# The start of gate and up in a hybrid block: one wait and the order of two scaled rows

## The reference

```python
x = x + jnp.einsum('bse,ed->bsd', y, w_out[l])

h = rmsnorm(x, norm_ffn[l])
f = jax.nn.silu(jnp.einsum('bsd,df->bsf', h, w_gate[l])) * jnp.einsum('bsd,df->bsf', h, w_up[l])
x = x + jnp.einsum('bsf,fd->bsd', f, w_down[l])
return rmsnorm(x, norm_final)
```

## Time and profile before

| | us |
|---|---|
| median of 3 runs | 1904.69 |
| lowest and highest run | 1904.26, 1906.11 |
| span of the profiled execution, first to last instruction | 1902.7 |
| TensorE busy in it | 1875.1 |
| VectorE, ScalarE, GpSimd busy | 1106.6, 808.4, 1144.9 |

### The profile page before, as it was taken

The page is one execution under the profiler, slowest core; times in us unless marked ns, Lnnn a source line. Parts: engine busy times, 40 slices in busy tenths (PEclk is TensorE's granted clock), DMA queues, the critical chain, the costliest instruction groups (busy, mean ns, idle before and its releaser), DMA issues.

```text
span 1902.7 us, 22499 instructions
## 1 busy us (share of the span) xinstructions
PE 1875.1 (99%) x8374; PEld 1544.2 (81%) x8374; DVE 1106.6 (58%) x1269; ACT 808.4 (42%) x938; POOL 1144.9 (60%) x427
## 2 busy tenths in 40 slices
PE   9999999999999999999999999999999999999998
PEld 7888788877788788888888788888888888888886
DVE  6899988997645755455545854445443025433535
ACT  6466766585643533333333433333333222232235
POOL 3577477945734465666655755555555676676663
PEclk9999999999999999999999999999999999999999
DMA  6222132265777334533355433323333765655455
GB/s 196 78 79 88 45 100 78 75 224 172 247 240 231 117 125 127 153 119 127 112 153 176 151 105 114 106 88 105 115 105 127 288 225 190 210 189 211 166 198 221
DMA packets 240946, 284.20 MB, mean 149 GB/s; under 512 B 12095, under 2 KB 166207, under 8 KB 240364
## 3 DMA queue, kind: packets, MB, share of 16 engines
q1 hardware_dynamic: 240874, 283.25, 44.8%
q10 hardware_dynamic: 2, 0.00, 0.0%
HBM read 200.90 MB, written 82.31 MB: 149 GB/s over the span
## 4 chain that ended last, share of the span: by engine, by line
PE 82%; POOL 6%; DVE 5%; ACT 2%; issue 2%; DMA 2%; POOLq 0%; SPq 0%; DVEq 0%; ACTq 0%
PE ps L2133 19%; PE ps L2135 19%; PE ps L2134 19%; PE acc L2133 8%; PE acc L2135 8%; PE acc L2134 8%; DVE a_lo L1863 1%; POOL nsq L877 1%; PE ps L2161 1%; DVE t_sum L1887 1%; POOL nsq L879 1%; POOL w_lo L804 1%; POOL f_lo L1018 0%; DVE wo_lo L1707 0%; POOL glu L827 0%
## 5 line engine op out<-in xcount | busy, mean ns | idle before, releaser
L933 POOL TENSOR_TENSOR t_lo<-t_sum,t_hi 128x2048 fp32r<-128x2048 f32 x44 | 205.6, 4674 | 165.3 <-ACT t_hi L1366 165.2
L927 POOL TENSOR_TENSOR b_lo<-m_raw,b_hi 128x1536 fp32r<-128x1536 f32 x44 | 157.6, 3582 | 179.2 <-ACT b_hi L1361 121.9
L1018 POOL TENSOR_TENSOR f_lo<-f_raw,f_hi 128x2048 fp32r<-128x2048 f32 (+1 forms) x42 | 182.2, 4338 | 129.3 <-ACT f_hi L1518 124.8
L2133 PE MATMUL ps<-h_hi,w_hi 128*128 128x512 f32 x512 | 201.1, 393 | 0.8 <-POOL w_lo L804 0.8
L2135 PE MATMUL ps<-h_hi,w_lo 128*128 128x512 f32 x512 | 199.4, 389 | 0.0
L2134 PE MATMUL ps<-h_lo,w_hi 128*128 128x512 f32 x512 | 199.2, 389 | 0.0
L1887 DVE TENSOR_TENSOR t_sum<-m_raw 128x512 f32<-128x512 f32 x88 | 141.7, 1630 | 97.4 <-PE acc L2135 87.6
L1518 ACT CAST f_hi<-f_raw 128x2048 fp32r<-128x2048 f32 (+1 forms) x42 | 74.3, 1769 | 263.6 <-PE ps L2135 168.1
L2133 PE MATMUL ps<-wd_hi,f_hi 128*128 128x512 f32 x462 | 179.8, 389 | 0.8 <-POOL wd_lo L1025 0.8
L2134 PE MATMUL ps<-wd_lo,f_hi 128*128 128x512 f32 x462 | 179.7, 389 | 0.0
L2135 PE MATMUL ps<-wd_hi,f_lo 128*128 128x512 f32 x462 | 179.7, 389 | 0.0
(11 more groups left out here) (257 smaller groups left out, 4689.1 us busy)
## 6 DMA issues: line engine op xcount, KB each, us to landing
f_raw<-f_scr SPq DMA_DIRECT2D x35, 1024.0 KB, 4.9
wd_raw<-in_w_down SPq DMA_DIRECT2D x60, 512.0 KB, 6.6
f_scr<-fs SPq DMA_DIRECT2D x110, 256.0 KB, 2.1
m_raw<-in_w_gate SPq DMA_DIRECT2D x88, 256.0 KB, 3.9
m_raw<-in_w_up SPq DMA_DIRECT2D x88, 256.0 KB, 5.1
w_raw<-in_w_in SPq DMA_DIRECT2D x32, 512.0 KB, 5.3
f_scr<-gt SPq DMA_DIRECT2D x44, 256.0 KB, 2.0
xt<-in_x SPq DMA_DIRECT2D x16, 512.0 KB, 6.3
```

The costliest lines, as they stand in the source:

```text
L927: g.tensor_tensor(b_lo[b][:, :, :, :], m_raw[b][:, 0:3], f32(b_hi[b][:, :, :, :]), ALU.subtract).then_inc(s_mlo, 1)
L933: g.tensor_tensor(t_lo[b][:, :, :, :], t_sum[b][:, :, :, :], f32(t_hi[b][:, :, :, :]), ALU.subtract).then_inc(s_mlo, 1)
L1018: g.tensor_tensor(f_lo[j % 3][:, 0:n], f_raw[j % 2][:, 0:n], f32(f_hi[j % 3][:, 0:n]), ALU.subtract).then_inc(s_dlo, 1)
L2133: pe.matmul(bank, lhs[0](c), rhs[0](c), start=first, stop=False, skip_group_check=more)
```

## The change

Five edits in the lists above. GpSimd waits for VectorE's `a_low(4)` and `a_low(5)` before `b_lo` of matrix 1. VectorE scales row 14 before `sum11` (at the end of the loop over rows, behind `a_low(3)`), does `a_low(4)` and `a_low(5)` back to back, and scales row 15 behind them. ScalarE casts `a_high(6)` before it copies row 14 out. TensorE turns row 14 in the same place as before, but row 15 behind product 5 and not ahead of it. Nothing is added to or taken from the work itself.

```diff
--- before.py
+++ after.py
@@ -1032,6 +1032,7 @@
                     if h:
                         gate_block(first, FI, behind=A_LO_DVE[1, 4])
                     elif i == 0:
+                        pool.wait_ge(s_alo_dve, A_LO_DVE[0, 5])
                         raw_lo(1, 1)
                         pool.wait_ge(s_t, 8)
                         a_low(6)
@@ -1473,8 +1474,8 @@
                     raw_hi(m + 1, 1, i + 1)
                 copy_p5(m, i, 0, first)
                 if starts == 0:
+                    a_high(6)
                     h2_copy(NT - 2)
-                    a_high(6)
                 silu(i, 0, h)
                 copy_u2(m, i, 0, first)
                 if starts == 1:
@@ -1918,6 +1919,7 @@
                     add_row(w, first_weight_sums if w == NT - 1 else lambda: norm_between(w))
                 if w == NT - 1:
                     a_low(0, 3)
+                    row_scaled(NT - 2)
                 if w == 3:
                     row_scaled(2)
                 if w == 1 or 3 <= w < NT - 2:
@@ -1994,10 +1996,9 @@
 
                 if first and not b:
                     sum11(m, i, b, h, first)
-                    row_scaled(NT - 2)
-                    a_low(0, early[0])
+                    for n in early:
+                        a_low(0, n)
                     row_scaled(NT - 1)
-                    a_low(0, early[1])
                     dve.wait_ge(s_hn, NT)
                     for n in range(2):
                         dve.wait_ge(s_x2st[n], 16 * NT // 2)
@@ -2410,6 +2411,8 @@
                             between(n)
                         matrix_product(n, m + b, i, b, None if b else new_half, first)
                     if b == 0:
+                        if between:
+                            between(0)
                         matrix_product(0, m + 1, i, 1, None, first)
                     elif not last:
                         matrix_product(0, m + 2, i + 1, 0, next_half)
@@ -2417,8 +2420,10 @@
 
             def last_rows(n):
 
-                if n in (4, 5):
-                    turn_h2(NT - 6 + n)
+                if n == 4:
+                    turn_h2(NT - 2)
+                if n == 0:
+                    turn_h2(NT - 1)
                 if n == 2:
                     for e in range(2):
                         pe.wait_ge(s_outf[e], NT)
```

## The result

The changed kernel takes 1908.39 us (median of 21 runs, 1904.98 to 1912.31), the kernel before, run beside it, 1906.27 us (21 runs, 1903.57 to 1908.52). The ratio is 1.0013, interval 1.0007 to 1.0019. That is some 2 us slower (2.1 between the medians, 2.3 between the means), under 0.2%. The forecast was 1904.9, from 1902.7 to 1907.6, on the three runs then known.

What follows compares the result with a forecast made beforehand. TensorE, busy 1875.1 of 1902.7 us, bounds the kernel, with 4.94 us of holes here. The gain at product 4 is paid back at products 3, 5 and 6: +0.17 on 1904.69, forecast 1904.9, range 1902.7 to 1907.6.

Steps and rivals of the forecast that it cites:

- The turns and their sum: VectorE and GpSimd alternate under an exclusive lock; the reordered chain to a_lo6 makes product 6 0.17 us later.
- product 6: TensorE waits behind a_lo6 after product 0 of matrix 1: one hole of some 3.0 us, until 649.76.
- The hole before product 3: Product 3 of matrix 0 waits for sum11, now behind row 14: a new hole of 0.9 us.
- product 5: Product 5 of matrix 0 waits for ScalarE's copy of u2: 0.4 us of hole.
- row 15 held beside b_lo: Row 15's scaling waits its turn beside GpSimd's b_lo, over 3 us; rival, not held: 1903.7, chance 0.10.
- a_lo6 as the last link: a_lo6 on GpSimd, behind the weight sums, ends at 649.70 and releases product 6 0.06 us later.
- the covers of b_lo and of matrix 2: Slack before delays reach TensorE: 2.7 us for b_lo of matrix 1, 4.97 us for matrix 2.
- All later work moves by the same 0.17: Everything behind product 6 shifts by 0.17 us, so the whole span of 1902.7 grows by just that.
- The first rival: TensorE's clock falls in the longer hole before product 6, costing 1.7 or 3.15 us: 1906.6 to 1908.1, chance 0.34.

Runs made afterwards that it cites:

- before_fill: Kernel before with unread matmuls in its two holes, ten before product 4 and five before product 6: 1906.82 us, ratio 1.0001.
- nr_before: Kernel before, with GpSimd's b_lo of matrix 24, at the second half's start, waiting for VectorE's last sum of hidden values: 1904.24 us, ratio 0.9990.
- nr_after: Changed kernel, with GpSimd's b_lo of matrix 24, at the second half's start, waiting for VectorE's last sum of hidden values: 1904.10 us, ratio 0.9989.
- wait_only2: Kernel before with only GpSimd's added wait from the change, rows 14 and 15 in their old order, second run: 1907.38 us, ratio 1.0007.
- wait_only: Kernel before with only GpSimd's added wait from the change, rows 14 and 15 in their old order: 1906.95 us, one run.
- order_only: Changed kernel without GpSimd's wait, only the new order of rows 14 and 15 on VectorE, ScalarE and TensorE: 1907.30 us, ratio 1.0005.
- before_again: Kernel before once more, unchanged: 1905.00 us, ratio 0.9996.
- nr_fill: Kernel before with b_lo of matrix 24 waiting for VectorE's last hidden sum, and unread matmuls in three TensorE holes: 1903.70 us, ratio 0.9987.

## Why the prediction was wrong

- **The turns and their sum** were right: forecast +0.17 us at product 6, measured 0.08 (from the start of t_lo, 651.34 - 625.99 against 649.59 - 624.32). The hole before product 3 (0.9 forecast, 0.83), product 5 (0.4, 0.56), product 6 (about 3.0, 2.57), row 15 held beside b_lo (4.54 us), a_lo6 as the last link, the covers of b_lo and of matrix 2: as forecast. VectorE and GpSimd took turns (row 15's 4.54 us here against 1.28, the sum's 3.97 against 0.68 at 1080), as the Trainium skill's SBUF — State Buffer, section "SBUF: two separate sides", has it.
- **The step that failed** is "All later work moves by the same 0.17". A hole at 1085 us, shut in both profiles of the kernel before, is open in all three of the changed kernel. That it also opens in part of the executions of the kernel before is inferred, from before_fill's profile and from the time that nr_before gains. The open hole wasn't in the one profile at hand, and my covers ended with matrix 2, at 666 us. The rows that would have warned were there: b_lo started 0.7 us after the start of VectorE's last sum (1080.06 against 1079.35), just as that ended, behind a clock that had just fallen.
- **The first rival** was right as a mechanism: of nine profiles with the long hole before product 6 (the first two lines of the table) four show the fall behind it, at 1.4 to 1.8 us (forecast 1.7): from t_lo to the next hole it takes 1066.42 - 626.89 = 439.5 us in nr_after and 437.7 in the changed kernel, 439.2 in wait_only2 and 437.8 in wait_only. The length of the hole doesn't tell the two kinds apart: 2.58 to 2.71 us with a fall behind it, 2.57 to 2.72 without. It alone is not the loss: nr_after has it and is as fast as nr_before. That the measured 1908.39 lies so near the 1908.1 that this rival allowed is chance; its fall gives some 0.7 us of it, as estimated below. The Trainium skill's advice on long idle gaps (TensorE: Matmul & The Clock Gate, "Why this matters for your kernels") fits with four in nine, not with every execution.
- **The sizes fit, as an estimate.** Suppose that the kernel before has the hole in half of its executions (four of the eight profiles in the last line of the table, which are of six kernels) and the changed one in all. Then the difference is half of what the open hole costs over the fall that keeps it shut. That is 413.71 less 410.61 in seven of eight profiles, 412.16 less 410.61 in one, so about 1.5 us. With 0.1 from the seam and four ninths of 1.4 to 1.8 behind product 6 it is 2.2 to 2.4 us; measured are 2.1 to 2.5 (medians, ratio), with an interval of 1.3 to 3.6. The other pair fits too: with the hole forced open in both, the changed kernel is 0.0006 slower, 1.1 us, within the error of the two runs. In nr_after the fall behind product 6 is offset by the missing one at 1074.
- **The range** ended at 1907.6. It was built round 1904.69, the median of three runs; over 21 runs the same kernel has 1906.27. Had I taken 1.85 us of spread as a doubt of the middle, not only of single runs, the range would have held. Of the 3.5 us between forecast and result 1.6 are this middle (1906.27 less 1904.69), the rest is what the change costs beyond the forecast 0.17.
- **Shown and not shown.** Shown: the place of the loss (by deciding the race both ways), and the wait's part in moving the hole. Likely, on few profiles: that the long hole before product 6 keeps the clock from falling at 1074 (0 of 7 against 4 of 8), and that 1.6 us of work between the two undoes this (2 of 2). The seven matmuls also move the hole at 1074 away from everything else ahead of them, so that it is this pair of holes that counts is not shown, nor how the chip relates two holes 423 us apart. And whether the order of the rows has a small part of its own stays open: order_only's 1.0005 fits both.

## What to carry to other kernels

Where two engines take turns, moving a wait only moves the idle time; so ask what the idle time does where it now lies. Before, a clock that fell in the first hole was paid for by the second hole (before_again), while one long hole at the end of the chain has nothing behind it to take it up. And look along the whole program for races decided by less than a microsecond, because an edit far ahead can tip how often they are lost. Here one wait on GpSimd that decides such a race was worth 0.9990, and the new order of the seam nothing.

## What the runs showed of the hardware that was not expected

- A lower clock made a stretch of an execution faster: behind the hole at 1074 a stretch at 0.5, costing 1.6 us, kept a hole of 2.8 us shut, 410.61 us against 412.16 or 413.71. Fastest was neither, 409.01 us in nr_after.
- Idle gaps of the same length are followed by a fall of the clock in some executions and not in others (2.40 to 2.44 us at 1074: 6 of 17 profiles counting both kinds in the table), and whether they are can hang on a place far ahead: with a hole of over 2.5 us 423 us earlier it was 0 of 7, with 7 matmuls more between the two holes 2 of 2.
- The times of one kernel spread over 5 us (1903.57 to 1908.52 in 21 runs), where three runs had shown 1.85. The falls and the race are part of it, not all: t_lo starts at 623.69 to 626.89 in the profiles, ahead of the seam and the race, and nr_fill, with the holes filled and the race decided, still spreads over 3.4 us.
